# Hybrid attention and retention block: buffers for two tiles of x, an earlier second weight panel, the norm weights as a wide product

## The chip, the cores and the metric

The kernel runs on one core of a Trainium2 chip. The metric is the device time of one execution in microseconds (us), less is better. Before the change it takes 1588.69 us, the median of three runs (1588.14 to 1590.66).

## The reference

One residual layer over x of shape (1, 2048, 1024), float32. Cut to what matters:

```python
h = rms_norm(x, norm_gain)                       # x * rsqrt(mean(x*x) + eps) * norm_gain
aq, ak, av, ag, rq, rk, rv, rg = split(h @ w_in) # 1024 columns in, eight groups out
attn = window_attention(aq, ak, av, ...)         # 16 heads of 64, 4 kv heads, RMS norm on q and k,
                                                 # chunks of 64, window of 2 chunks, a sink per head
ret  = retention(rq, rk, rv, ...)                # 8 heads, chunks of 64, a state carried along the
                                                 # sequence, group norm per head
mixed = concat(attn * silu(ag), ret * silu(rg))  # 2048 wide
return x + mixed @ w_out                         # 2048 rows of 1024
```

Everything in it is computed in full; outputs are float32.

## The kernel before, in words

**Precision.** Each float32 operand of a projection is split into a high part H and a low part L (`fp32r`), and each product is three TensorE passes: H by H (L1441), L by H and H by L (L1442, L1443). Of a tile of x, ScalarE makes the high part (`xh`, L715) and VectorE the low part (`xl`, L1153); of a weight, ScalarE makes the high part (`wh1`, L531) and GpSimd the low part (`wl1`, L387). The norm weights (`ngain`) are applied in `xh` and `xl` as a scale per partition, so both work on one 128x128 piece at a time, 8 pieces a tile. The factor 1/rms of each row is applied later, at the eviction of a projection; `xsq` squares and sums the rows of x on ScalarE (L697), `xms_` and `xpow` make the power on VectorE and GpSimd, `XB` transposes it on TensorE.

**Tiling.** Four blocks of 512 rows (tiles t = 0 to 3 of 128 rows), and in each four head units, so units n = 0 to 15. A unit has 20 jobs of 24 matmuls each (`job(n, j)`): 0 to 3 make q, k and v for one tile each, with a tile of x as the moving or stationary side (384 wide, weight panel 0); 4 to 7 the gates and the retention's q and k (panel 1; they need all four tiles of x), 8 to 11 the retention's v and gate (panel 2), 12 to 19 the output projection (panel 3). Three PSUM banks go round among the jobs. Between the jobs stand the small pieces of the two mixers: `TQ` transposes q and k of a tile after their norm (L1460), `S_` makes scores (L1476), `PT` and `PV` the transposed probabilities and their product with v (L1500), `A` and `I` the retention inside a chunk with its state (L1538 to L1540), `MT` the transposed retention output.

**Weights.** In block 0 each panel comes from DRAM in four chunks through `stage` (three buffers, and `sx` for the fourth chunk of the first panel). A chunk is split by `wh1` and `wl1` (two steps each, numbered s = 0 to 7 in a panel), then `save` writes both parts to scratch in DRAM, and later blocks only `reload` them. `load(q)` waits on `s_wl`, the count of finished `wl1` steps, until its buffer is free.

**x.** The transposed tile lies in `xt[:, t % 2]`, two buffers, so tiles 2 and 3 wait for `xl` of tiles 0 and 1. `first_rows(t)` brings the untransposed rows of block 0 into `acc`. In block 0 all DMA starts are issued by SyncE's queue (SP) in a written order: norm weights, x and weight chunks in turn, tile 1, rows 0, identity; then tile 2 (waits), rows 1, tile 3 (waits), the gains of q and k, `attention_constants` (bias and the sinks), `load(4)`, rows 2, `load(5)`, rows 3, `load(6)`, `load(7)`, the saves.

**Order.** The order on every engine is written out by hand, unit by unit (GpSimd from L434, ScalarE from L718, VectorE from L1158, TensorE from L1564). An engine takes its instructions strictly in that order, so a wait of one holds all behind it. TensorE's order begins: job(0,0), job(0,1), job(0,2), TQ(0,0), job(0,3), S_(0,0), job(0,4), TQ(0,1), XB(0), job(0,5). ScalarE's: the first weight panel between the pieces of tile 0, tiles 1 and 2 with `xsq(0,0)` and `xsq(0,1)` between, the eviction `qkv(0,0)`, tile 3, and only then `wh1` of panel 1. VectorE's `carry_in(0)` stands ahead of `qk_norm(0,0)` and reads the sinks.

Of the kernel before, what the change touches and what calls it, by code (L numbers as in the profile page):

```python
# [94 lines left out]
def build(nc, x, norm_gain, q_gain, k_gain, sinks, ret_gain, xT, wp0, wp1, wp2, wp3, c_bias, c_ret, c_ident, out):  # L95
# [9 lines left out]
    with ExitStack() as ctx:  # L105
# [272 lines left out]
        def _(pool):  # L378
# [62 lines left out]
            ggm(0, 0); wl1(1, 0, 3); ggm(0, 1); wl1(1, 0, 4); mixl(0, 2); wl1(1, 0, 5); wl1(1, 0, 6)
            wl1(1, 0, 7); mixl(0, 3); gpow(0, 0); ggm(0, 2); wl1(0, 3, 0); wl1(0, 3, 1); wl1(0, 3, 2)
            wl1(0, 3, 3); gpow(0, 1); ggm(0, 3); wl1(0, 3, 4)

            rpow(1, 0); wl1(0, 3, 5); wl1(0, 3, 6); wl1(0, 3, 7); gpow(0, 2); rpow(1, 1); rpow(1, 2)
            wl1(1, 1, 0); gpow(0, 3); wl1(1, 1, 1); wl1(1, 1, 2); rpow(1, 3); wl1(1, 1, 3); wl1(1, 1, 4)
            wl1(1, 1, 5); wl1(1, 1, 6); wl1(1, 1, 7); wl1(1, 2, 0); wl1(1, 2, 1); wl1(1, 2, 2); wl1(1, 2, 3)
# [1283 lines left out]
```

## Time and profile before

| | before |
|---|---|
| median of three runs | 1588.69 us |
| profiled execution | 1589.65 us |
| its span | 1587.9 us |
| TensorE busy | 1560.4 us (98%) |
| VectorE busy | 1113.1 us (70%) |
| ScalarE busy | 853.2 us (54%) |
| GpSimd busy | 451.4 us (28%) |
| mean DMA rate | 204 GB/s |

The span is the stretch that the profile covers; the execution's own time is 1.75 us longer. A busy share is an average over all stages. In the views, PE is TensorE, DVE is VectorE, ACT is ScalarE, POOL is GpSimd, SPq is SyncE's queue of DMA starts; L and a number is the line of the kernel before. In a timeline row the columns are the start and the duration in us, the engine, line and operation, output and inputs with shapes, the count; in square brackets how long the engine stood idle before it and what ended that. Where an operation has a count above one, the duration is of the whole run of them.

### The profile page before, as it was taken

How to read it: one execution, taken by the hardware profiler on the slowest of the kernel's cores; microseconds unless marked ns; L12 is line 12 of the kernel's file. 1: busy time of each engine (PE TensorE's matmuls, PEld its weight loads, DVE VectorE, ACT ScalarE, POOL GpSimd, SP SyncE). 2: the span in 40 equal slices, each digit the busy share in tenths (PEclk: the TensorE clock that was granted, in tenths of full speed). 3: DMA queues.
4: the chain of work that ended last, by engine and by line, in shares of the span. 5: the costliest groups of instructions: out<-in, count | busy, mean ns of one | idle time of the engine just before them, and what ended most of it. 6: DMA issues, size and time to landing. Idle time of an engine off the chain costs nothing.

```text
span 1587.9 us, 24908 instructions
## 1 busy us (share of the span) xinstructions
PE 1560.4 (98%) x8120; PEld 1354.2 (85%) x8120; DVE 1113.1 (70%) x2934; ACT 853.2 (54%) x2421; POOL 451.4 (28%) x453
## 2 busy tenths in 40 slices
PE   6899999999999999999999999999999999999999
PEld 5798888978889888898888989889898888988887
DVE  6879587796946758576775766857587584775764
ACT  7766565655635355454754645546474454535641
POOL 5565566643312021120212212121120211202210
PEclk9999999999999999999999999999999999999999
DMA  7987495755874445553556635526447455444451
GB/s 260 330 315 280 175 345 186 285 208 178 323 256 166 188 146 188 186 209 145 186 215 225 247 128 195 205 99 247 168 159 282 148 197 189 149 179 156 154 207 54
DMA packets 123328, 323.66 MB, mean 204 GB/s; under 512 B 16832, under 2 KB 60224, under 8 KB 123200
## 3 DMA queue, kind: packets, MB, share of 16 engines
q1 hardware_dynamic: 123200, 322.07, 55.5%
q8 instruction: 66, 1.08, 0.3%
q14 instruction: 62, 0.51, 0.1%
HBM read 250.72 MB, written 71.30 MB: 203 GB/s over the span
## 4 chain that ended last, share of the span: by engine, by line
PE 84%; DVE 9%; issue 3%; ACT 2%; DMA 1%; POOL 1%; SPq 0%; DVEq 0%; POOLq 0%; ACTq 0%
PE jb L1441 24%; PE jb L1443 24%; PE jb L1442 24%; PE ob L1500 2%; PE s L1476 2%; PE ptb L1485 2%; PE ob L1460 1%; PE s L1539 1%; DMA stage<-wp_dram 1%; PE s L1538 1%; DVE hTL L1153 1%; PE ab L1550 1%; DVE acc L1139 1%; PE s L1377 1%; DVE qS L955 1%
## 5 line engine op out<-in xcount | busy, mean ns | idle before, releaser
L1441 PE MATMUL jb<-wH,hTH 128*128 128x512 f32 (+1 forms) x1024 | 376.6, 368 | 9.4 <-POOL wL L387 9.4
L1442 PE MATMUL jb<-wL,hTH 128*128 128x512 f32 (+1 forms) x1024 | 372.6, 364 | 0.0
L1443 PE MATMUL jb<-wH,hTL 128*128 128x512 f32 (+1 forms) x1024 | 372.3, 364 | 0.0
L1441 PEld LDWEIGHTS jb<-wH,hTH 128*128 128x128 f32 x1024 | 193.3, 189 | 30.0 <-POOL wL L387 11.9
L1443 PEld LDWEIGHTS jb<-wH,hTL 128*128 128x128 f32 x1024 | 193.3, 189 | 20.5
L1442 PEld LDWEIGHTS jb<-wL,hTH 128*128 128x128 f32 x1024 | 193.7, 189 | 17.6
L1441 PE MATMUL jb<-wH,mxH 128*128 128x512 f32 x512 | 207.6, 405 | 0.0
L1441 PE MATMUL jb<-hTH,wH 128*128 128x512 f32 x512 | 202.7, 396 | 2.8 <-POOL wL L387 2.8
L1443 PE MATMUL jb<-wH,mxL 128*128 128x512 f32 x512 | 200.6, 392 | 0.0
L1442 PE MATMUL jb<-wL,mxH 128*128 128x512 f32 x512 | 200.3, 391 | 0.0
L1442 PE MATMUL jb<-hTL,wH 128*128 128x512 f32 x512 | 199.7, 390 | 0.0
L1443 PE MATMUL jb<-hTH,wL 128*128 128x512 f32 x512 | 199.5, 390 | 0.0
L589 ACT ACTIVATE sx<-sx,nm 128x128 f32<-128x128 f32 x256 | 99.9, 391 | 160.9 <-DVE d L988 160.7
L412 POOL TENSOR_TENSOR mxL<-mixr,mxH 128x256 fp32r<-128x256 f32 x64 | 47.8, 747 | 465.4 <-ACT mxH L651 464.3
L387 POOL TENSOR_TENSOR wL<-stage,wH 128x512 fp32r<-128x512 f32 (+1 forms) x126 | 156.5, 1265 | 68.3 <-ACT wH L531 68.0
L1441 PEld LDWEIGHTS jb<-hTH,wH 128*128 128x128 f32 x512 | 96.2, 188 | 22.9 <-POOL wL L387 4.5
L1443 PEld LDWEIGHTS jb<-wH,mxL 128*128 128x128 f32 x512 | 96.1, 188 | 21.0
L1443 PEld LDWEIGHTS jb<-hTH,wL 128*128 128x128 f32 x512 | 96.1, 188 | 20.7
L1442 PEld LDWEIGHTS jb<-hTL,wH 128*128 128x128 f32 x512 | 96.3, 188 | 18.1
L1442 PEld LDWEIGHTS jb<-wL,mxH 128*128 128x128 f32 x512 | 96.6, 189 | 16.5
L1441 PEld LDWEIGHTS jb<-wH,mxH 128*128 128x128 f32 x512 | 96.3, 188 | 16.5
L394 POOL TENSOR_TENSOR rstd<-ms,mhalf 128x5 f32<-128x5 f32 x64 | 75.9, 1186 | 113.6 <-DVE ms L932 113.5
(142 smaller groups left out, 3016.6 us busy)
## 6 DMA issues: line engine op xcount, KB each, us to landing
wH<-scrH SPq DMA_DIRECT2D x144, 512.0 KB, 7.0
wL<-scrL SPq DMA_DIRECT2D x144, 512.0 KB, 7.9
stage<-wp_dram SPq DMA_DIRECT2D x48, 512.0 KB, 6.6
scrH<-wH SPq DMA_DIRECT2D x48, 512.0 KB, 6.5
scrL<-wL SPq DMA_DIRECT2D x48, 512.0 KB, 7.5
wH<-scrH SPq DMA_DIRECT2D x48, 384.0 KB, 5.5
wL<-scrL SPq DMA_DIRECT2D x48, 384.0 KB, 6.6
out_dram<-acc SPq DMA_DIRECT2D x16, 512.0 KB, 2.8
```

The lines of the kernel that those rows point to most:

```text
L387: pool.tensor_tensor(wL[b][:, s, 0:w], stage_of(at // 2, w)[:, s % 2], wH[b][:, s, 0:w].bitcast(F32), ALU.subtract).then_inc(S["s_wl"], 1)
L394: pool.tensor_tensor(rstd[:, t % 2], ms[:, t % 2], mhalf[:, 0:5], ALU.pow).then_inc(S["s_rstd"], 1)
L412: pool.tensor_tensor(mxL[:, 0:2, cols], mixr[:, :, :], mxH[:, 0:2, cols].bitcast(F32), ALU.subtract).then_inc(S["s_mixl"], 1)
L589: act.activation(v, v, ACT.Exp, bias=nm4[:, t % 2, i:i + 1], accum_out=den[:, t % 2, i:i + 1])
L955: v.scalar_tensor_tensor(out=qS[other, t % 2, :, a * 64:a * 64 + 64], in0=tr[rows, 0:256].rearrange("p (c q) -> p c q", q=64), scalar=qkg[ ...
L1139: v.tensor_tensor(a, a, bank_of(n, J_OUT + i)[:, :], ALU.add).then_inc(S["s_acc"], 1)
L1441: pe.matmul(o, lh, rh_, start=i == 0, stop=False)
L1442: pe.matmul(o, lh, rl_, start=False, stop=False)
L1443: m = pe.matmul(o, ll, rh_, start=False, stop=i == last)
L1476: m = pe.matmul(s_parts[:, par, hp], qS[:, t % 2, 2 * hp + par], kHL[:, :, win], start=True, stop=True)
L1485: m = pe.transpose(ptb[:, i * P:(i + 1) * P], sx[:, at:at + P], ident[:, :])
L1500: m = pe.matmul(o, v, pT[:, par * 256:(par + 1) * 256].rearrange("p (r q) -> p r q", q=64), start=i == 0, stop=i == 1)
```

## The change

- Tiles 2 and 3 of block 0 get own buffers (`xt23`, in the memory that `mxL` takes later), so their DMAs wait for nothing.
- For all tiles but the first, VectorE multiplies the tile by the norm weights in place (`xg`, two instructions of 128x512 a tile); `xh` is then a plain copy, and `xl` a plain subtraction, two of 128x512 each. Tile 0 keeps the old form.
- The four chunks of the first panel are started from ScalarE's queue, ahead of its first activation. SP's order is new: rows 0 to 3 and loads 4 to 6 come ahead of the gains and the attention constants; load 6 waits only for the first `wl1` pair.
- Panel 1 of unit 0 is split directly behind panel 0 on GpSimd (seven of its eight steps), on ScalarE between the pieces of x; TensorE runs job(0,0) to job(0,4) without anything between, then TQ(0,0), XB(0).
- The orders of all engines in all units are new. In TensorE's, units 6, 7, 9, 10, 11, 13, 14 and 15 have job(n,2) ahead of I(n-1,3); in unit 15, TQ(15,1) stands behind job(15,4) and I(15,2) behind job(14,13); unit 8 keeps its order there.

```diff
+        with nc.sbuf_tensor("xt23", [P, 2, KT, P], F32) as xt23:
+            pass
+        mxL, mxH = sb("mxL", [P, 4, BLK], F32R), sb("mxH", [P, 4, BLK], F32R)
+        def x_tile(b, t):
+            return xt23[:, t - 2] if b == 0 and t >= 2 else xt[:, t % 2]
...
             def load(q):
-                if q >= STAGES + 1:
-                    sp.wait_ge(S["s_wl"], 2 * (q - STAGES) + 2)
+                if q > STAGES:
+                    sp.wait_ge(S["s_wl"], 2 * (0 if q == 6 else q - STAGES) + 2)
...
             for c in range(4):
                 sp.dma_start(xt[:, 0, 2 * c:2 * c + 2], xT[0, 0, :, 2 * c:2 * c + 2]).then_inc(s_xp[c], 16)
-                load(c)
             x_turned(0, 1)
             first_rows(0)
+            x_turned(0, 2)
             sp.dma_start(ident[:, :], c_ident).then_inc(S["s_ident"], 16)
-            x_turned(0, 2)
+            load(6)
             first_rows(1)
+            load(4)
             x_turned(0, 3)
-            qk_gains()
+            load(5)
+            first_rows(2)
+            first_rows(3)
+            for half in range(2):
+                rows = slice(half * HD, half * HD + HD)
+                sp.dma_start(qkg[rows, 0:1], q_gain.rearrange("(d o) -> d o", o=1)).then_inc(S["s_qkg"], 16)
+                sp.dma_start(qkg[rows, 1:2], k_gain.rearrange("(d o) -> d o", o=1)).then_inc(S["s_qkg"], 16)
             attention_constants(0)
-            load(4)
-            first_rows(2)
-            load(5)
-            first_rows(3)
-            load(6)
             load(7)
...
# ScalarE
+                act.wait_ge(S["s_xg"], 8 * b + 2 * (t - 1) + c + 1)
+                ks = slice(4 * c, 4 * c + 4)
+                act.activation(hTH[:, ks, t * P:(t + 1) * P], x_tile(b, t)[:, ks], ACT.Copy).then_inc(S["s_xH"], 1)
+            for q in range(4):
+                act.dma_start(stage_of(q, W_WIDTH[0]), wp[0][0, :, 2 * q:2 * q + 2, :]).then_inc(s_stage(q), 16)
...
             xh(0, 0, 0); wh1(0, 0, 0); wh1(0, 0, 1); xh(0, 0, 1); wh1(0, 0, 2); wh1(0, 0, 3); xh(0, 0, 2)
+            wh1(0, 0, 4); wh1(0, 0, 5); xh(0, 0, 3); wh1(0, 0, 6); wh1(0, 0, 7); xsq(0, 0); xh(0, 1, 0)
+            xsq(0, 1); xh(0, 1, 1); wh1(0, 1, 0); wh1(0, 1, 1); xh(0, 2, 0); wh1(0, 1, 2); wh1(0, 1, 3)
+            wh1(0, 1, 4); xh(0, 2, 1)
+            qkv(0, 0); xsq(0, 2); wh1(0, 1, 5); xsq(0, 3); xh(0, 3, 0); wh1(0, 1, 6); xh(0, 3, 1); wh1(0, 1, 7)
...
# VectorE
+            def xg(b, t, c):
+                part = x_tile(b, t)[:, 4 * c:4 * c + 4]
+                v.tensor_tensor(part, part, ngain[:, 4 * c:4 * c + 4].unsqueeze(2).broadcast_to([P, 4, P]), ALU.mult
+                                ).then_inc(S["s_xg"], 1)
+            xl(0, 0, 0); xl(0, 0, 1); xl(0, 0, 2); xl(0, 0, 3); xg(0, 1, 0); xg(0, 1, 1); xl(0, 1, 0)
+            xg(0, 2, 0); xl(0, 1, 1); xms_(0, 0); xg(0, 2, 1); xl(0, 2, 0); xl(0, 2, 1); xg(0, 3, 0)
+            xg(0, 3, 1); xl(0, 3, 0); xl(0, 3, 1); xms_(0, 1); carry_in(0); v_parts(0, 0); xms_(0, 2)
...
# GpSimd
+            wl1(0, 0, 7); wl1(0, 1, 0); xpow(0, 0); wl1(0, 1, 1); wl1(0, 1, 2); wl1(0, 1, 3); wl1(0, 1, 4)
+            wl1(0, 1, 5); wl1(0, 1, 6); xpow(0, 1); xpow(0, 2)
+            rpow(0, 0); xpow(0, 3); rpow(0, 1); wl1(0, 1, 7); rpow(0, 2); rpow(0, 3); wl1(0, 2, 0); wl1(0, 2, 1)
...
# TensorE
-            job(0, 0); job(0, 1); job(0, 2); TQ(0, 0); job(0, 3); S_(0, 0); job(0, 4); TQ(0, 1); XB(0)
-            job(0, 5); S_(0, 1); TQ(0, 2); job(0, 6); S_(0, 2); TQ(0, 3); PT(0, 0); job(0, 7); S_(0, 3)
+            job(0, 0); job(0, 1); job(0, 2); job(0, 3); job(0, 4); TQ(0, 0); XB(0); job(0, 5); TQ(0, 1)
+            S_(0, 0); job(0, 6); TQ(0, 2); S_(0, 1); job(0, 7); TQ(0, 3); S_(0, 2); PT(0, 0); job(0, 8)
...
-            job(6, 0); I(5, 2); MT(5, 0); job(6, 1); I(5, 3); job(6, 2); TQ(6, 0); MT(5, 1); job(6, 3)
+            job(6, 0); I(5, 2); MT(5, 0); job(6, 1); job(6, 2); I(5, 3); TQ(6, 0); MT(5, 1); job(6, 3)
...
-            job(15, 0); I(14, 2); MT(14, 0); job(15, 1); I(14, 3); MT(14, 1); job(15, 2); TQ(15, 0); job(15, 3)
-            TQ(15, 1); MT(14, 2); job(15, 4); S_(15, 0); MT(14, 3); TQ(15, 2); job(15, 5); S_(15, 1); TQ(15, 3)
+            job(15, 0); I(14, 2); MT(14, 0); job(15, 1); job(15, 2); MT(14, 1); I(14, 3); TQ(15, 0); job(15, 3)
+            job(15, 4); TQ(15, 1); MT(14, 2); S_(15, 0); job(15, 5); TQ(15, 2); MT(14, 3); S_(15, 1); job(15, 6)
```

## Rows read from the trace of the kernel before

**Rows 1.** Windows by stage: length, busy us per engine, granted clock, DMA share, GB/s.
```profile
0.00:45.00 45.00, 31.36 (x141) 26.35 (x142) 31.90 (x82) 34.13 (x91) 26.71 (x29) 0.96 0.79 274
45.00:100.00 55.00, 51.82 (x271) 43.50 (x270) 45.96 (x91) 34.84 (x96) 32.79 (x32) 1.00 0.84 297
100.00:500.00 400.00, 397.39 (x2090) 345.73 (x2090) 303.12 (x749) 228.29 (x633) 194.04 (x176) 1.00 0.68 248
500.00:1460.00 960.00, 957.85 (x5000) 834.06 (x4999) 652.46 (x1799) 501.16 (x1445) 177.78 (x195) 1.00 0.50 184
1460.00:1588.00 128.00, 121.99 (x626) 104.61 (x624) 79.69 (x217) 54.81 (x158) 20.10 (x23) 0.99 0.40 151
```
**Rows 2.** Waits of TensorE, 0 to 45 us: total us, times, longest.
```profile
PE jb L1441 <- POOL wL L387: 11.4, 7, 8.1
```
**Rows 3.** Timeline of TensorE, 8 to 45 us.
```profile
15.84 0.33 PE L1441 MATMUL jb<-wH,hTH 128*128 128x384 f32 x1
...
23.99 0.34 PE L1443 MATMUL jb<-wH,hTL 128*128 128x384 f32 x1
26.60 0.90 PE L1460 MATMUL ob<-ident,rawqn 128*128 128x128 f32 x3 [2.28 <-DVE rawqn L946]
27.16 0.67 PE L1441 MATMUL jb<-wH,hTH 128*128 128x384 f32 x1
...
30.05 0.34 PE L1441 MATMUL jb<-wH,hTH 128*128 128x384 f32 x1
...
43.49 0.47 PE L1441 MATMUL jb<-hTH,wH 128*128 128x512 f32 x1
```
**Rows 4.** Timeline of GpSimd, first run of weight steps.
```profile
7.06 6.06 POOL L387 TENSOR_TENSOR wL<-stage,wH 128x384 fp32r<-128x384 f32 x6 [6.22 <-ACT wH L531]
```
**Rows 5.** Timeline of VectorE, 0 to 45 us.
```profile
7.65 8.71 DVE L1153 SCALAR_TENSOR_TENSOR hTL<-xt,ngain,hTH 128x128 fp32r<-128x128 f32 x12 [1.43 <-ACT hTH L715]
...
25.45 0.17 DVE L915 TENSOR_SCALAR nsink<-sink 128x2 f32<-128x2 f32 x1 [3.74 <-DMA sink<-sink_logits_dram]
```
**Rows 6.** Timeline of ScalarE, 16 to 32 us.
```profile
18.30 1.04 ACT L697 ACTIVATE gate<-acc 128x1024 f32<-128x1024 f32 x1
...
27.19 1.15 ACT L531 ACTIVATE wH<-stage 128x512 fp32r<-128x512 f32 x2 [3.71 <-DMA stage<-wp_dram]
```
**Rows 7.** Timeline of SyncE's queue, start of `load(4)`.
```profile
21.94 0.59 SPq L317 DMA_DIRECT2D stage<-wp_dram  x1
```
**Rows 8.** Window of 9 to 12 us, columns as in Rows 1.
```profile
9.00:12.00 3.00, 3.00 (x11) 2.46 (x9) 3.00 (x4) 2.72 (x8) 3.00 (x4) 1.00 1.03 417
```
**Rows 9.** Groups by line and form: count, duration ns min/median/max, start of first and last.
```profile
L715 ACT ACTIVATE hTH<-xt,ngain x128: 384/388/410, 5.1 to 1175.5; 128x128 fp32r<-128x128 f32 x128
...
L1153 DVE SCALAR_TENSOR_TENSOR hTL<-xt,ngain,hTH x128: 333/344/1449, 5.6 to 1177.4; 128x128 fp32r<-128x128 f32 x128
...
L899 DVE TENSOR_TENSOR pTL<-ptb,pTH x64: 675/684/693, 63.4 to 1554.9; 128x512 fp32r<-128x512 f32 x64
```
**Rows 10.** Timeline of TensorE, 45 to 75 us.
```profile
73.48 0.36 PE L1500 MATMUL ob<-pTH,veven 128*128 128x256 f32 x1 [1.22 <-DVE mixr L1028]
```
**Rows 11.** Timeline of VectorE, 45 to 60 us.
```profile
53.84 1.21 DVE L988 TENSOR_TENSOR d<-nm,sink 128x4 f32<-128x4 f32 x1
```
**Rows 12.** Timeline of TensorE, unit 6 and unit 8.
```profile
597.25 0.34 PE L1443 MATMUL jb<-wH,hTL 128*128 128x384 f32 x1
597.83 0.35 PE L1538 MATMUL s<-rst,zst 128*128 128x256 f32 x1 [0.24 <-issue]
...
795.71 0.36 PE L1538 MATMUL s<-rst,zst 128*128 128x256 f32 x1 [0.28 <-issue]
```
**Rows 13.** Timeline of VectorE around 597 us.
```profile
597.09 0.42 DVE L899 TENSOR_TENSOR aL<-amr,aH 128x256 fp32r<-128x256 f32 x1
```
**Rows 14.** Timeline of TensorE, unit 15.
```profile
1480.59 0.52 PE L1460 MATMUL ob<-ident,rawqn 128*128 128x128 f32 x3 [0.71 <-DVE kHL L960]
...
1537.16 0.36 PE L1538 MATMUL s<-rst,zst 128*128 128x256 f32 x1 [1.13 <-DVE kwL L899]
```

More of the change, by code:

```diff
@@ L441, in _ @@
[L441 to L447, printed above, removed]
@@ L789, in _ @@
-            gnx(5, 1); rvg(5, 3)
-            qkv(6, 0); kwh_ah(5, 3); ocopy(5, 2); v_shift(6, 0); rh(5, 3); mth(5, 0); qkv(6, 1); gnx(5, 2)
-            v_shift(6, 1); rh(6, 0); qkv(6, 2); ocopy(5, 3); tqh(6, 0); mth(5, 1); xsq(2, 2); v_shift(6, 2)
-            xsq(2, 3); qkv(6, 3); gnx(5, 3); tqh(6, 1); v_shift(6, 3); mth(5, 2); exps(6, 0); tqh(6, 2)
+                    for k in (2 * c, 2 * c + 1):
+                        i = act.activation(hTH[:, k, 0:P], x_tile(b, t)[:, k], ACT.Copy, scale=ngain[:, k:k + 1])
@@ new lines, in _ @@
+            pth(0, 3); gnx(0, 0); wh1(0, 3, 2); wh1(0, 3, 3); wh1(0, 3, 4); mixh(0, 2); kwh_ah(0, 2)
+            ocopy(0, 1); rh(0, 2); rvg(0, 3); wh1(0, 3, 5); obcopy(0, 3)
+            qkv(1, 0); mth(0, 0); gnx(0, 1); mixh(0, 3); v_shift(1, 0); rh(0, 3); ocopy(0, 2); kwh_ah(0, 3)
+            qkv(1, 1); wh1(0, 3, 6); mth(0, 1); wh1(0, 3, 7); v_shift(1, 1); gnx(0, 2); tqh(1, 0); ocopy(0, 3)
+            qkv(1, 2); wh1(1, 1, 0); wh1(1, 1, 1); wh1(1, 1, 2); wh1(1, 1, 3); v_shift(1, 2); xsq(1, 0)
@@ new lines, in _ @@
+            qkv(5, 0); mth(4, 0); ocopy(4, 2); v_shift(5, 0); qkv(5, 1); gnx(4, 2); v_shift(5, 1); xsq(2, 0)
+            qkv(5, 2); ocopy(4, 3); mth(4, 1); tqh(5, 0); xsq(2, 1); v_shift(5, 2); rh(5, 0); qkv(5, 3)
+            gnx(4, 3); v_shift(5, 3); tqh(5, 1); mth(4, 2); exps(5, 0); tqh(5, 2); mth(4, 3); exps(5, 1)
+            tqh(5, 3); pth(5, 0); exps(5, 2); obcopy(5, 0); pth(5, 1); ag(5, 0); exps(5, 3); ag(5, 1)
+            mixh(5, 0); obcopy(5, 1); rqh(5); pth(5, 2); mixh(5, 1); rqz(5); rk(5); obcopy(5, 2); mixh(5, 2)
@@ new lines, in _ @@
+            rvg(5, 0); pth(5, 3); kwh_ah(5, 0); rvg(5, 1); obcopy(5, 3); ocopy(5, 0); kwh_ah(5, 1); rh(5, 1)
+            mixh(5, 3); rvg(5, 2); gnx(5, 0); kwh_ah(5, 2); ocopy(5, 1); rh(5, 2); gnx(5, 1); rvg(5, 3)
+            qkv(6, 0); kwh_ah(5, 3); ocopy(5, 2); rh(5, 3); v_shift(6, 0); mth(5, 0); qkv(6, 1); gnx(5, 2)
+            v_shift(6, 1); qkv(6, 2); xsq(2, 2); ocopy(5, 3); v_shift(6, 2); tqh(6, 0); mth(5, 1); xsq(2, 3)
+            rh(6, 0); qkv(6, 3); gnx(5, 3); v_shift(6, 3); tqh(6, 1); mth(5, 2); exps(6, 0); tqh(6, 2)
@@ L830, in _ @@
[L830 to L831 removed]
+            qkv(10, 0); kwh_ah(9, 3); ocopy(9, 2); rh(9, 3); v_shift(10, 0); mth(9, 0); qkv(10, 1); gnx(9, 2)
+            v_shift(10, 1); qkv(10, 2); xsq(3, 2); ocopy(9, 3); v_shift(10, 2); tqh(10, 0); mth(9, 1); xsq(3, 3)
+            rh(10, 0); qkv(10, 3); gnx(9, 3); v_shift(10, 3); tqh(10, 1); mth(9, 2); exps(10, 0); tqh(10, 2)
@@ new lines, in xl @@
+            def xl(b, t, c):
+                v.wait_ge(S["s_xH"], x_done(b, t, c))
+                if b == t == 0:
+                    for k in (2 * c, 2 * c + 1):
+                        i = v.scalar_tensor_tensor(out=hTL[:, k, 0:P], in0=x_tile(b, t)[:, k], scalar=ngain[:, k:k + 1],
+                                                   in1=hTH[:, k, 0:P].bitcast(F32), op0=ALU.mult, op1=ALU.subtract)
+                    i.then_inc(S["s_xL"], 1)
+                    return
+                ks, cols = slice(4 * c, 4 * c + 4), slice(t * P, (t + 1) * P)
+                sub(hTL[:, ks, cols], x_tile(b, t)[:, ks], hTH[:, ks, cols]).then_inc(S["s_xL"], 1)
```

867 lines of the change are left out of this document (423 added, 444 removed).

## The prediction, made before the changed kernel ran

> **What bounds the kernel now.** I read the windows by stage first. TensorE is busy 957.85 of 960 us from 500 to 1460, and 397.39 of 400 before that [rows 1]. So work removed from other engines is worth nothing as such; only TensorE's idle time can be won: 13.64 us in the first 45 us, 3.18 from 45 to 100, 2.61 from 100 to 500, 2.15 from 500 to 1460, and 6.01 after 1460, part of it behind the last matmul. In the first 45 us the waits view gives 11.4 us to the weight low parts of GpSimd, 8.1 of them ahead of the first matmul and 3.3 in six later ones [rows 2]. The TensorE timeline has the other large wait, 2.28 us ahead of TQ(0,0), said to be for the normed q [rows 3]. VectorE's timeline says what it was: the instruction `nsink` stood 3.74 us for the sinks' DMA [rows 5], and all behind it on VectorE with it. After that wait TensorE was slow: from 27.16 to 30.05 nine matmuls of 384 columns take 0.32 us each, while from 15.84 to 23.99 forty-seven take 0.173 each [rows 3]. The granted clock, whose mean over the first stage is 0.96 [rows 1], stands at half of its 2.4 GHz there; nine times 0.148 is 1.3 us. The steady state loses a little in each unit at one place: I(n-1,3) starts 0.58 us after the matmul before it, where 0.17 is normal [rows 12], because `aL`, which it reads, ends at 597.51 [rows 13]. In unit 15 two waits of 0.71 and 1.13 idle us stand [rows 14].
>
> **Start, up to job(0,5): 3.2 us gained.** The first matmul depends on x chunk 0 and weight chunk 0. Both were issued by 2.3 us and the engines of the DMA moved what they could from 3 us on; I leave the start at 8.11. Eight steps of job(0,0) at GpSimd's pace of 1.01 us [rows 4] end at 15.84 as before. Then jobs 1 to 4 have nothing between, so what counts is when x and panel 1 are ready.
> The path: ScalarE has `xsq(0,1)` ahead of `xh(0,1,1)`, and it needs rows 1. Ahead of their last byte stand 4.8 MB (tile 0, four weight chunks of 0.39, tile 1, rows 0, tile 2, load 6, rows 1, 0.52 each). At 417 GB/s [rows 8] from 3 us they end at 14.5; at the stage's mean of 274 [rows 1] from 1 us at 18.4. I take the middle, 16.4. Then, with 1.1 us for a square [rows 6], 0.58 for a copy or weight split 512 wide (1.15 for two [rows 6]) and 0.69 for a 512 wide subtraction [rows 9]: xh(0,1,1) 18.1, xl(0,1,1) 18.8. The second half of job(0,1) is due at 17.9: 0.9 late. Load 4 lands 1.26 later than rows 1, tile 3 and load 5 behind it at 20.2; two splits, xh(0,2,0) 19.8, three splits from 20.2 to 21.9, xh(0,2,1) 22.5, its xl 23.2: job(0,2), from 20.9, has its half at 23.0, 0.2 late, and ends at 25.3. ScalarE goes on with qkv(0,0), 1.1 us by width, two squares and one split between: xh(0,3,0) 27.0, xl(0,3,0) 27.7. So job(0,3) waits 2.4 us, a new wait of about the old one's length, and I charge it the old one's slow clock, 1.3. It ends at 27.7 + 24 x 0.173 + 1.3 = 33.2; job(0,4) (24 of 0.173 x 512/384) at 38.7. The steps of GpSimd for panel 1, seven of 1.35 from 15.7, are done by 26: the 3.3 us of late low parts in job(0,4) go, and so does the wait for load 4, that was issued at 21.94 [rows 7] and left ScalarE idle 3.71 us [rows 6]. With TQ(0,0) and XB job(0,5) starts at 39.3 against 43.49 [rows 3]; 1.0 us of small TensorE work (S_(0,0), TQ(0,1)) has moved behind it: 3.2 gained. Bounds: with no wait but GpSimd's, job(0,4) ends at 33.9, gain 8; with rows 1 at 18.4 and xl(0,3,0) at 30, and VectorE and GpSimd holding each other up by 1.5 more, a gain of 0, and below it -1 for a second drop of the clock.
> The x work itself: ScalarE's 128 pieces of 388 ns become 8 and 30 wide ones of 0.58, 49.7 us against 20.5; VectorE's 128 of 344 (44) become 8, 30 products and 30 subtractions of 0.69 (44) [rows 9]. Both engines are idle enough after 100 us, so it is nothing there; the price in the first 30 us is in the path above. Twelve pieces took 8.71 us beside GpSimd's weight steps, 0.73 each against 0.344 alone [rows 5, 9]; a wide one takes that wait once rather than four times. By the Trainium skill, SBUF — State Buffer, section "SBUF: two separate sides", a VectorE instruction with two SBUF inputs and a GpSimd instruction that reads SBUF hold a shared port in turn, each for its whole length. The trace agrees: such pieces go at GpSimd's pace. Taken strictly, a wide instruction in that stretch waits for the rest of the GpSimd step that is under way.
>
> **ScalarE's queue.** It saves SyncE four starts of 0.4 to 0.6 us, so tile 1 is asked for some 2 us earlier, and they cost ScalarE as many, before its first input is there (idle until then): nothing, unless the chunks now compete with more of x. Bounds: 0.5 gained, 1 lost; I take 0. By the Trainium skill, DMA: Bandwidth & Descriptors, section "Issuing engines are not separate DMA queues", another issuing engine saves no more than the issue time. No run here shows a second issuer.
>
> **45 to 100 us: 1.2 gained of 3.18.** The wait at 73.48, 1.22 for `mixr` [rows 10], is VectorE's: it is busy 45.96 of 55 us [rows 1] and some tiny instructions take 1.21 us there beside GpSimd [rows 11]. Panel 1 has gone from GpSimd by then, so these get shorter, but tile 0's softmax, once in the first 45 us, now falls in. Bounds: -5 and +3.
>
> **100 to 500: 1.3 of 2.61.** Waits of TQ and PV for VectorE, in units whose TQ is now later by a job or so. Bounds -1.5 and +2.5.
>
> **500 to 1460 and after: 2.9.** I counted seven units (6, 7, 9, 10, 11, 13, 14) with I(n-1,3) behind job(n,1), each with a gap of 0.41. A job of 4.16 us now stands between, against which `aL` at 597.51 has ended long before; 7 x 0.41 = 2.9. Against it stands unit 8: it had the new order already and still has an idle 0.28 at 795.71 [rows 12], since VectorE had x pieces and the state update ahead of `aL`. If VectorE's new orders do the same the term is 0. They put fewer instructions ahead, so I take it whole.
>
> **After 1460: 1.8 of 2.3.** The same gap in unit 15, 0.4; TQ(15,1) gets a job before it (0.71), I(15,2) another (1.13) [rows 14]. I leave 0.4 to a new wait. Bounds 0 and 2.5.
>
> **Sum.** 3.2 + 1.2 + 1.3 + 2.9 + 1.8 = 10.4 off the profiled execution's 1589.65: 1579.3. That execution lies 0.96 above the median of the runs, so by the median it is 1578.3. I forecast 1579.
>
> **Rivals.**
> (a) Only the order of TensorE's late pieces pays. Evidence: the first 45 us are bound by the DMA (0.79 share, 417 GB/s where it peaks [rows 1, 8]), and moving rows ahead moves x back. The start gives 0, 45 to 500 gives 0.5, the rest 4.7: -5.2, 1584. Against it: the waits at 21.94 to 27 are SyncE's order, not the rate.
> (b) All early waits go: 8 + 2.5 + 2 + 2.9 + 2.2 = 17.6, 1572. For it: the bytes suffice if rows 1 land at 14.5 and ScalarE's squares fit. Against it: five ScalarE instructions stand between qkv(0,0) and tile 3.
> (c) Slower: VectorE becomes the bound from job(0,5) to 100 us. TQ(0,0) comes 12 us later than at 26.60, so the softmax of tile 0 (four wide ones of 0.68 and five small ones, up to 1.21 each beside GpSimd, 5.8 in all) and 1.3 of q and k fall behind 45 us, where VectorE has 9.0 idle, and that in pieces between TensorE's results. If none is usable TensorE is 7.1 later, with two slow stretches of 1.3: 9.7; the 1.2 and 1.3 of the next terms are lost. 3.2 + 2.9 + 1.8 - 9.7 = -1.8, and with the start at 0 it is -5: 1591 to 1594, say 1592. It decides once VectorE's waits in that stretch exceed the present ones by 8. Against it: the softmax of before didn't stand on TensorE's path there.
> (d) No change: the start gives 0 and VectorE's order brings unit 8's wait to every unit; what is left is the 1.8 at the end, less something: 1587.5.
>
> **How the numbers follow.** Forecast 0.46, (a) 0.19, (b) 0.11, (c) 0.12, (d) 0.12. The band of 0.2% (about what a measurement of this kernel can tell from no change) is 3.2 us, 1585.5 to 1591.9. The forecast, (b) and most of (a) are below it: 0.74. (d) and a part of (a) and (c) are in it: 0.17. The rest of (c) is slower: 0.09. The range, 1573.5 to 1588, takes in the forecast's bounds, (a) and half of (d), and leaves out (c) and the far end of (b).
>
> **What would show it.** Right: in the new trace job(0,5) starts near 39.3; a wait of about 2.4 ahead of job(0,3) ended by VectorE's or ScalarE's tile 3, and matmuls of 0.52 after it; none for the low parts in job(0,4); I(n-1,3) of units 6 to 14 without idle time. Wrong: rows 1 landing after 19 us, waits of TensorE for VectorE over 5 us between 45 and 100, or idle time unchanged at I(n-1,3).

## The result and the profile after

The changed kernel takes 1573.5 us (median of four executions, 1573.34 to 1574.11) against 1589.6 for the kernel before beside it (1588.14 to 1590.66): ratio 0.9898, 95% interval 0.9882 to 0.9914. It is 16.1 us faster, where the forecast's sum was 10.4, and 1573.5 lies on the lower edge of the range. The sign was right and the term for the start was near; the other four terms were each too small by 1.4 us or more.

The windows of the changed kernel by stage (columns as in [rows 1]):

```profile
0.00:45.00 45.00, 32.02 (x150) 27.50 (x151) 33.35 (x62) 28.81 (x65) 30.92 (x31) 1.00 0.90 324
45.00:100.00 55.00, 54.14 (x299) 47.34 (x298) 48.40 (x105) 37.11 (x104) 35.35 (x32) 1.00 0.83 299
100.00:500.00 400.00, 398.08 (x2109) 348.97 (x2108) 308.60 (x744) 231.22 (x623) 192.22 (x176) 1.00 0.67 247
500.00:1460.00 960.00, 960.00 (x5024) 839.67 (x5024) 663.84 (x1783) 490.23 (x1407) 183.25 (x198) 1.00 0.51 186
1460.00:1572.00 112.00, 107.79 (x546) 91.59 (x545) 70.40 (x182) 45.91 (x134) 16.11 (x18) 1.00 0.36 135
```

From 500 to 1460 us TensorE is now busy all 960 us, where 2.15 were idle, and yet more than 2.15 us were gained there. That is the first thing to see. TensorE's records overlap: a matmul of 0.33 us is followed by the next after 0.17. So the idle time before a late one is about 0.16 us less than what it loses. The starts are the better measure. In both kernels the jobs stand in the same order; this table has the start of the first matmul of some jobs, read from both timelines:

| job | before | after | difference |
|---|---|---|---|
| (0,0) | 8.11 | 9.89 | +1.78 |
| (0,3) | 27.16 | 29.09 | +1.94 |
| (0,4) | 33.40 | 33.52 | +0.12 |
| (0,5) | 43.49 | 39.78 | -3.71 |
| (0,9) | 74.93 | 67.47 | -7.47 |
| (1,2) | 106.42 | 100.39 | -6.03 |
| (2,0) | 194.73 | 190.44 | -4.28 |
| (5,1) | 496.69 | 487.95 | -8.73 |
| (6,0) | 587.80 | 579.11 | -8.69 |
| (15,0) | 1459.67 | 1446.56 | -13.11 |
| last job's end | 1584.11 | 1567.79 | -16.31 |

At the marks from (0,3) to (0,9) less small work has been done in the changed kernel than before; at the others both have done the same. The gain falls between (1,2) and (2,0): the changed kernel has three new waits there.

TensorE's timeline of the changed kernel, the places that answer to [rows 3] (L1469 to L1471 are now the three passes):

```profile
9.89 0.69 PE L1469 MATMUL jb<-wH,hTH 128*128 128x384 f32 x1 [9.89 <-POOL wL L396]
...
18.62 0.44 PE L1469 MATMUL jb<-wH,hTH 128*128 128x384 f32 x1 [0.36 <-DVE hTL L910]
...
29.09 0.41 PE L1469 MATMUL jb<-wH,hTH 128*128 128x384 f32 x1 [1.88 <-DVE hTL L910]
...
39.78 0.48 PE L1469 MATMUL jb<-hTH,wH 128*128 128x512 f32 x1
...
117.50 0.52 PE L1488 MATMUL ob<-ident,rawqn 128*128 128x128 f32 x3 [1.01 <-DVE kHL L973]
119.05 0.50 PE L1469 MATMUL jb<-wH,mxH 128*128 128x512 f32 x1 [0.56 <-ACT rawqn L550]
...
128.09 0.50 PE L1469 MATMUL jb<-wH,mxH 128*128 128x512 f32 x1 [0.35 <-DVE acc L1152]
```

The start is 1.8 us late, job(0,3) waits 1.88 us for tile 3, and none of job(0,4)'s four waits for GpSimd is left. The last three rows are the new waits. The rows of ScalarE and VectorE say why the start and job(0,3) are late:

```profile
6.27 1.28 ACT L723 ACT_TABLE_LOAD   x1 [6.27 <-DMA xt<-xT_dram]
...
16.59 0.63 ACT L728 ACTIVATE hTH<-xt 128x512 fp32r<-128x512 f32 x1 [2.23 <-DVE xt L1170]
...
18.17 0.61 ACT L728 ACTIVATE hTH<-xt 128x512 fp32r<-128x512 f32 x1
...
26.62 0.61 ACT L728 ACTIVATE hTH<-xt 128x512 fp32r<-128x512 f32 x1
```

```profile
23.78 3.49 DVE L1170 TENSOR_TENSOR xt<-xt,ngain 128x512 f32<-128x512 f32 x2
27.27 3.37 DVE L910 TENSOR_TENSOR hTL<-xt,hTH 128x512 fp32r<-128x512 f32 x2
...
770.65 1.29 DVE L1170 TENSOR_TENSOR xt<-xt,ngain 128x512 f32<-128x512 f32 x2
```

The first part of x, which landed at 3.80 us before, is there at 6.27. The four chunks of weights are now started from 0.73 us on from another queue, beside and partly ahead of it; the first experiment shows that this is the reason. A wide product takes 0.65 us at 770, where GpSimd has no weight step, and 1.74 at 23.78 beside its weight steps.

I(5,3) starts 0.17 us behind the last matmul of job(6,2), where it started 0.58 behind that of job(6,1) [rows 12]:

```profile
592.72 0.33 PE L1471 MATMUL jb<-wH,hTL 128*128 128x384 f32 x1
592.89 0.28 PE L1566 MATMUL s<-rst,zst 128*128 128x256 f32 x1
593.01 0.28 PE L1567 MATMUL s<-rv,aH 128*128 128x256 f32 x1
```

### The profile page after: what moved, and what is told of

Same layout as the page of the kernel before. It is cut to its first block, busy times and chain, and to the rows that moved or that the text cites. A ratio compares the mean times of both kernels' runs of the same rounds, so it can differ in the third digit from the quotient of the medians.

```text
span 1571.6 us, 24771 instructions
## 1 busy us (share of the span) xinstructions
PE 1552.0 (99%) x8120; PEld 1355.1 (86%) x8120; DVE 1124.6 (72%) x2874; ACT 833.3 (53%) x2331; POOL 457.9 (29%) x453
## 4 chain that ended last, share of the span: by engine, by line
PE 92%; DVE 4%; POOL 1%; DMA 1%; issue 1%; ACT 1%; SPq 0%; DVEq 0%; ACTq 0%; POOLq 0%
PE jb L1469 26%; PE jb L1470 26%; PE jb L1471 26%; PE ob L1528 2%; PE s L1504 2%; PE ptb L1513 2%; PE ob L1488 1%; PE s L1567 1%; PE ab L1578 1%; PE s L1566 1%; POOL wL L396 1%; PE s L1405 1%; DMA stage<-wp_dram 1%; PE ab L1405 0%; PE ab L1407 0%
## 5 line engine op out<-in xcount | busy, mean ns | idle before, releaser
L1469 PE MATMUL jb<-wH,hTH 128*128 128x512 f32 (+1 forms) x1024 | 376.3, 367 | 13.0 <-POOL wL L396 10.7
L1471 PE MATMUL jb<-wH,hTL 128*128 128x512 f32 (+1 forms) x1024 | 372.3, 364 | 0.0
L1469 PEld LDWEIGHTS jb<-wH,hTH 128*128 128x128 f32 x1024 | 193.0, 188 | 33.6 <-POOL wL L396 12.4
L1471 PEld LDWEIGHTS jb<-wH,hTL 128*128 128x128 f32 x1024 | 193.1, 189 | 20.4
L1469 PE MATMUL jb<-wH,mxH 128*128 128x512 f32 x512 | 207.1, 405 | 0.9 <-ACT rawqn L550 0.6
L1469 PE MATMUL jb<-hTH,wH 128*128 128x512 f32 x512 | 201.4, 393 | 0.0
L1471 PE MATMUL jb<-wH,mxL 128*128 128x512 f32 x512 | 200.6, 392 | 0.0
L1471 PE MATMUL jb<-hTH,wL 128*128 128x512 f32 x512 | 199.7, 390 | 0.0
L1471 PEld LDWEIGHTS jb<-wH,mxL 128*128 128x128 f32 x512 | 96.2, 188 | 21.1
L1471 PEld LDWEIGHTS jb<-hTH,wL 128*128 128x128 f32 x512 | 96.2, 188 | 20.5
L1469 PEld LDWEIGHTS jb<-hTH,wH 128*128 128x128 f32 x512 | 96.3, 188 | 18.9 <-ACT rawqn L550 0.3
L1469 PEld LDWEIGHTS jb<-wH,mxH 128*128 128x128 f32 x512 | 96.4, 188 | 18.2 <-ACT rawqn L550 0.8
```

The lines of the kernel that those rows point to most:

```text
L1469: pe.matmul(o, lh, rh_, start=i == 0, stop=False)
L1471: m = pe.matmul(o, ll, rh_, start=False, stop=i == last)
```

## The experiments

**The chunks back on SyncE's queue.**

```diff
             for c in range(4):
                 sp.dma_start(xt[:, 0, 2 * c:2 * c + 2], ...)
+                load(c)
-            for q in range(4):
-                act.dma_start(stage_of(q, W_WIDTH[0]), ...)
```

> The changed kernel, with the first four weight chunks started again by SyncE's queue, in turn with the four parts of tile 0, and none by ScalarE's. Theory (the chunks on ScalarE's queue are ahead of x part 0, whose landing went from 3.80 to 6.27 us, and that is what moved the first matmul from 8.11 to 9.89): the first matmul is at 8.1 again; but the path of tile 3 is set by ScalarE and by VectorE beside GpSimd, which all start 1.8 us earlier too, so the execution is 1.0 to 1.8 us shorter than the changed kernel, 1572. Rival (the chunks' place pays for itself, since the start then runs against the landing of rows 1 and tile 3): first matmul at 8.1, but the wait ahead of job(0,3) grows from 1.88 by as much, TensorE's clock falls again, and the time is 1573.5 or up to 1575.

Measured: 1574.32 us (1573.16 to 1574.85), not to be told from the changed kernel's. The first matmul is at 7.45 again, sooner even than the 8.1 of theory and rival; the time is the rival's. The first row of ScalarE, then rows of TensorE:

```profile
3.80 1.28 ACT L724 ACT_TABLE_LOAD   x1 [3.80 <-DMA xt<-xT_dram]
```

```profile
7.45 0.69 PE L1467 MATMUL jb<-wH,hTH 128*128 128x384 f32 x1 [7.45 <-POOL wL L397]
...
19.80 0.45 PE L1467 MATMUL jb<-wH,hTH 128*128 128x384 f32 x1 [1.26 <-DVE hTL L908]
...
25.14 0.44 PE L1467 MATMUL jb<-wH,hTH 128*128 128x384 f32 x1 [0.67 <-DVE hTL L908]
30.30 0.49 PE L1467 MATMUL jb<-wH,hTH 128*128 128x384 f32 x1 [2.80 <-DVE hTL L908]
```

The first matmul is 2.4 us sooner, and all of it is lost again in the middle of job(0,1) and of job(0,2) and ahead of job(0,3), which starts 1.2 us later than in the changed kernel, and with the clock at its lower level for part of it (granted clock 0.58 from 30 to 33 us). ScalarE's queue costs the first matmul 2.4 us and costs the kernel nothing that can be measured.

**I(n-1,3) back in its old place**, eight units.

```diff
-            job(6, 0); I(5, 2); MT(5, 0); job(6, 1); job(6, 2); I(5, 3); TQ(6, 0); ...
+            job(6, 0); I(5, 2); MT(5, 0); job(6, 1); I(5, 3); job(6, 2); TQ(6, 0); ...
```

> The changed kernel, with I(n-1,3) of units 6, 7, 9, 10, 11, 13, 14 and 15 put back between job(n,1) and job(n,2); nothing else. Theory (the place of I(n-1,3) is the whole of what the steady state gained): each of the eight units has its wait of 0.4 us again, the time is 8 x 0.40 = 3.2 us longer, 1576.7. Rival (the new orders of VectorE and ScalarE made aL come earlier): under 1 us longer, 1573.5 to 1574.5. Second rival (more than the wait hangs on it, since the switch between a job and a small piece costs TensorE something each time): 8 x 0.5 = 4 us or more.

Measured: 1578.07, 4.6 us longer, as much as the second rival says. From the start of job(6,0) to the end 4.7 come back: eight times about 0.53, and one new wait at 906 that loses 0.47. In unit 6:

```profile
588.89 0.34 PE L1471 MATMUL jb<-wH,hTL 128*128 128x384 f32 x1
589.52 0.36 PE L1566 MATMUL s<-rst,zst 128*128 128x256 f32 x1 [0.29 <-issue]
589.72 0.28 PE L1567 MATMUL s<-rv,aH 128*128 128x256 f32 x1
```

From start to start it is 0.63 us, 0.46 more than normal. The other 0.07 or so is inside I(5,3): behind the wait its second matmul starts 0.20 after the first, where it is 0.12 in the changed kernel. The second rival's reason, a price of each switch between a job and a small piece, isn't seen: the step from I(5,3) to job(6,2) takes no longer than the one from I(5,3) to TQ(6,0) in the changed kernel (0.12 both).

**The same move in the kernel before.**

```diff
-            job(6, 0); I(5, 2); MT(5, 0); job(6, 1); I(5, 3); job(6, 2); TQ(6, 0); ...
+            job(6, 0); I(5, 2); MT(5, 0); job(6, 1); job(6, 2); I(5, 3); TQ(6, 0); ...
```

> The kernel before, with only this changed in TensorE's order: in the same eight units I(n-1,3) (in unit 15 with MT(14,1)) stands behind job(n,2) instead of ahead of it. Theory: 8 x 0.40 = 3.2 us shorter than before, 1586.4, with no idle time at these places. Rival (the wait follows, as in unit 8 of the kernel before, which has this order and waited 0.28 idle us nevertheless): within 1 us of before, 1589. Against more than 3.2: the other units' orders are those of before.

Measured: 1594.69, slower: ratio 1.0028 (1.0018 to 1.0038). Neither theory nor rival. In most of the middle units the 0.4 goes and a wait ahead of TQ(n,1) comes that loses 0.24, so about 0.2 is gained. In unit 15 this comes:

```profile
1482.59 0.87 PE L1460 MATMUL ob<-ident,rawqn 128*128 128x128 f32 x3 [4.62 <-DVE kHL L960]
...
1484.97 0.63 PE L1441 MATMUL jb<-hTH,wH 128*128 128x512 f32 x1
```

VectorE's old order has the state and norm of I(14,3) ahead of the q and k statistics. I(14,3) came a job later, so these did too, and TQ(15,1) waited 4.62 us. The matmuls after it ran 0.43 apart instead of 0.23, the clock at its lower level (granted clock 0.50 from 1482 to 1488 us). So the move pays 0.5 a unit with the changed kernel's orders of the other engines, and less than nothing with the old ones.

This run shows one thing more. Up to unit 6 its code is that of the kernel before, and yet it takes 1.1 us less from job(2,0) to job(6,0) in its profile (391.9 for 393.1): the losses of the kernel before at 260 us (0.66) and at 407 us (0.30) aren't there. So differences of about 1 us in this stretch come from one execution to the next.

**x in narrow pieces again**, the norm weights as a scale.

```diff
-                act.activation(hTH[:, ks, ...], x_tile(b, t)[:, ks], ACT.Copy)
+                for k in range(4 * c, 4 * c + 4):
+                    i = act.activation(hTH[:, k, ...], x_tile(b, t)[:, k], ACT.Copy, scale=ngain[:, k:k + 1])
```

VectorE's product is left out, and its subtraction works on pieces again.

> The changed kernel, with the norm weights applied again inside the high and low parts of x, eight 128x128 pieces a tile on ScalarE and eight on VectorE, and no product of its own on VectorE; the orders stay. Theory (the wide form is bought for the blocks after the first and the start: ScalarE 1.6 us a tile instead of 1.2, VectorE pieces that each wait for a GpSimd step): in the first 30 us TensorE waits 2 us more ahead of jobs 1 to 3, elsewhere nothing: 1575.5. Rival (VectorE gains from the missing product, twelve wide instructions beside GpSimd in the start, each up to 1.7 us): the wait ahead of job(0,3) is gone, and the time is 1571.5. Third: the units before blocks 1 to 3 (3, 7, 11), where the kernel before had waits at 804 and 1191 us, get them back: another 0.5 to 1 us.

Measured: 1579.56 (1576.35 to 1581.77), 6 us longer, with executions 5.4 us apart. The profiled execution is the longest of them, 8.4 above the changed kernel's. By its starts 2.9 is there at job(0,9), near what the theory has, 0.1 in units 8 and 12 each, and 5.3 in unit 4, at one place that none of the three named. TensorE's row, then one of ScalarE's from before it:

```profile
405.24 0.35 PE L1563 MATMUL s<-rHL,rqH 128*128 128x256 f32 x1 [3.44 <-DVE aL L915]
```

```profile
390.54 1.15 ACT L541 ACTIVATE wH<-stage 128x512 fp32r<-128x512 f32 x2 [3.63 <-DMA stage<-wp_dram]
```

The weight chunk for which ScalarE stands here is issued at 384.44, in SyncE's order behind a tile of x that waits for the low parts; that is 2.1 us later than in the changed kernel, the shift of 2.9 taken off. VectorE then stands 4.83 us for ScalarE. It is not in every execution: the shortest, 1576.35, is 2.9 us above the changed kernel, which the start alone gives. That the narrow pieces start this chain is read from one trace, and not shown.

**Two buffers for x.**

```diff
         def x_tile(b, t):
-            return xt23[:, t - 2] if b == 0 and t >= 2 else xt[:, t % 2]
+            return xt[:, t % 2]
```

SyncE's order: tile 2 behind load 4, tile 3 behind rows 2.

> The changed kernel, with tiles 2 and 3 of block 0 in the two old buffers: their DMAs wait for the low parts of tiles 0 and 1, and stand in SyncE's order where that wait is short (tile 2 behind load 4, tile 3 behind rows 2). Theory (the own buffers are not what gains): in the changed kernel VectorE takes tile 2 at 18.49 us and tile 3 at 23.78, and the last low part of tile 0 is done at 15.1, of tile 1 at 19.8, so both tiles land in time or up to 1 us late; the first job behind them shifts by at most 1, and VectorE's pace behind job(0,5) takes that up: 1573.5 to 1574.5. Rival (the buffers matter): tile 2 lands at 18.5 or later, VectorE stands with xl(0,1,1) behind it, each of jobs 1 to 3 waits, two slow stretches of the clock: 1576 or more.

Measured: 1579.16, 5.7 longer, which is the rival's number. TensorE's rows, then ScalarE's:

```profile
22.27 0.45 PE L1466 MATMUL jb<-wH,hTH 128*128 128x384 f32 x1 [1.17 <-DVE hTL L910]
...
30.62 0.41 PE L1466 MATMUL jb<-wH,hTH 128*128 128x384 f32 x1 [1.81 <-DVE hTL L910]
...
35.44 0.69 PE L1466 MATMUL jb<-wH,hTH 128*128 128x384 f32 x1 [1.84 <-DVE hTL L910]
```

```profile
32.86 0.63 ACT L541 ACTIVATE wH<-stage 128x512 fp32r<-128x512 f32 x1 [3.70 <-DMA stage<-wp_dram]
```

VectorE gets the tiles at 20.9 and 26 us, some 2 later than in the changed kernel; job(0,3) starts 1.5 later for it. The larger part comes inside job(0,3), 4.1 us, and is made by what stands behind the waiting SyncE: load 7, issued at 27.56 instead of 23.33. ScalarE stands 3.70 us for it, with tile 3's second half behind, and TensorE's clock is at its lower level meanwhile (granted clock 0.50 from 33 to 37 us).

**The whole DMA side as before**, orders as changed.

```diff
             sp.dma_start(ident[:, :], c_ident).then_inc(S["s_ident"], 16)
-            load(6)
+            x_turned(0, 2)
             first_rows(1)
-            load(4)
             x_turned(0, 3)
...
             attention_constants(0)
+            load(4)
+            first_rows(2)
+            load(5)
+            first_rows(3)
+            load(6)
             load(7)
```

> The changed kernel with the whole DMA side of the start as before: two buffers for x, chunks on SyncE's queue in turn with x, tile 2 and 3 waiting, gains and constants ahead of loads 4 to 6. The orders of the engines and the wide product stay. Theory (what the early second panel is bought with is SyncE's order): load 4 is issued at about 22 us again and lands at 27, so ScalarE, which now has the splits of panel 1 ahead of tile 3, makes tile 3 only at 30 to 33, job(0,3) waits 6 to 8 us, and of this 3 to 6 us stay at the end: 1577 to 1580. Rival (VectorE's pace from job(0,5) to 70 us takes up even that): 1575 or less.

Measured: 1584.7, 11.2 longer, more than the theory had. Load 4 is issued at 25.25. The wait stands ahead of job(0,2) and not of job(0,3), since two splits of panel 1 are ahead of tile 2 in ScalarE's order. ScalarE's row, then TensorE's:

```profile
30.46 1.15 ACT L542 ACTIVATE wH<-stage 128x512 fp32r<-128x512 f32 x2 [10.80 <-DMA stage<-wp_dram]
```

```profile
33.04 0.69 PE L1464 MATMUL jb<-wH,hTH 128*128 128x384 f32 x1 [10.23 <-DVE hTL L908]
```

**The new DMA side in the kernel before.** The same edit the other way round, with the own buffers; the first chunks stay on SyncE's queue.

> The kernel before with the DMA side of the change alone: own buffers for tiles 2 and 3, SyncE's order with loads 4 to 6 and all rows ahead of the gains and constants; the first chunks stay on SyncE's queue, the orders of all engines and the narrow x pieces stay. The reverse of the run with the old DMA side. Theory (the DMA side removes the wait of ScalarE for load 4, 3.71 us, but TQ(0,0) stands ahead of job(0,3) and waits for the sinks, which are issued at about 20 us in either): the wait of 2.3 stays within 1 us, the 3.3 us of late low parts in job(0,4) shrink to under 1, total 2 to 4 us shorter than before, 1586. Rival (the DMA side is worth its 11.6 us here too, since it is what the start waits for): 1578. Second rival (VectorE's pace behind job(0,5) takes up the gain): 1588 to 1589.

Measured: 1587.14 against 1589.59 (ratio 0.9991, 0.9982 to 1.0000; executions 1585.49 to 1591.44): the theory's lower end at best. In its profile, that of the longest execution, 2.06 us are won at job(0,5) and kept, and 3.7 are lost in unit 8, where VectorE waits for the sinks' DMA and TensorE for VectorE:

```profile
787.19 0.17 DVE L924 TENSOR_SCALAR nsink<-sink 128x2 f32<-128x2 f32 x1 [4.43 <-DMA sink<-sink_logits_dram]
```

So the DMA side is worth 0 to 3 us with the old orders and 11 with the new; the parts of this change don't add.

**VectorE's carry_in later, in the kernel before.**

```diff
-            ... gnm(7, 1); carry_in(8); xl(2, 3, 0); ...
-            mtl(7, 0); qk_stats(8, 1); ...
+            ... gnm(7, 1); xl(2, 3, 0); ...
+            mtl(7, 0); carry_in(8); qk_stats(8, 1); ...
```

> The kernel before, with VectorE's carry_in(8) and carry_in(12), which read the sinks, behind mtl(7,0) and mtl(11,0), where the changed kernel has them (with the wait of qk_norm on s_mixr that the changed kernel has in its place); nothing else. In the kernel before, VectorE stands 1.97 us for the sinks' DMA at 787, and in the profile with the new DMA side 4.43, behind which TensorE waited 2.9 at 793 with a slow stretch: 3.7 us in one place. Theory (this wait, of a length that changes from one execution to the next, is a part of what the changed kernel gained in units 8 and 12, and why executions of the kernel before lie 5 us apart and those of the changed one 0.8): 0.5 to 1.5 us below before, 1588.5, with executions within 1.5 us of each other and less idle time at I(7,3) and I(11,3). Rival (the scatter comes from the start, where the clock falls or does not after the wait of 2.3): median and spread as before.

Measured: 1587.26 against 1589.78 (ratio 0.9984, 0.9975 to 0.9993), more than the theory had. By the starts 0.8 us are won in unit 8 and 0.2 in unit 12, where the waits of the kernel before are gone. Another 1.4 differ ahead of unit 5, where the same losses are missing as in the run with I(n-1,3) moved in the kernel before, whose code is unchanged there; so these need not be this edit's. Eight of eleven executions lie within 1.2 us, the others up to 2.5 above: the sinks are at most a part of the scatter.

**TQ(15,1) and I(15,2) back in their old places.**

```diff
-            job(15, 4); TQ(15, 1); MT(14, 2); S_(15, 0); job(15, 5); ...
+            TQ(15, 1); MT(14, 2); job(15, 4); S_(15, 0); job(15, 5); ...
-            job(14, 12); A(15, 3); PV(15, 1); job(14, 13); MT(15, 0); I(15, 2); ...
+            job(14, 12); A(15, 3); I(15, 2); PV(15, 1); job(14, 13); MT(15, 0); ...
```

> The changed kernel, with TQ(15,1) again right behind job(15,3) and I(15,2) right behind job(14,12). Theory: the two waits of before return, 0.87 and 1.29 us: 2.0 us longer, 1575.5. Rival (VectorE's new order of unit 15 has taken the waits away too): under 0.7 longer. Second rival (as in the kernel before with one piece moved, VectorE's order now does not match, and the wait of TQ(15,1) is 3 us or more with a slow stretch behind it): 1578 or more.

Measured: 1574.51, 1.0 longer, between theory and first rival. TQ(15,1) loses 0.53 again (0.87 before), PV(15,3) 0.35, and I(15,2) nothing where it had lost 1.29: the new orders of the other engines had taken that wait away already.

**TensorE's old order in units 2 and 3 alone.**

```diff
-            job(2, 0); I(1, 2); MT(1, 0); job(2, 1); job(2, 2); I(1, 3); MT(1, 1); job(2, 3); TQ(2, 0)
+            job(2, 0); job(2, 1); I(1, 2); MT(1, 0); job(2, 2); TQ(2, 0); MT(1, 1); job(2, 3); I(1, 3)
```

> The changed kernel with TensorE's order in units 2 and 3 as before (the other engines' orders as changed). From job(2,0) to job(4,0) the changed kernel takes 194.3 us and the kernel before 197.9. Theory (the gain of 100 to 500 us lies in TensorE's order, two small pieces side by side instead of each between two jobs, and later TQ): 2 to 3.6 us come back, 1576. Rival (as at unit 15: orders that don't match cost more than either): over 4 us, 1578 or more, with a wait of over 2 us somewhere. Second rival (the new order of VectorE makes it): under 1 us.

Measured: 1631.33, 58 us longer. TensorE's waits from 190 to 440 us (total, times, longest), the first four:

```profile
PE ob L1528 <- DVE pTL L910: 9.8, 2, 5.7
PE s L1504 <- DVE kHL L973: 8.7, 2, 4.5
PE ob L1488 <- DVE rawqn L959: 7.3, 2, 4.2
PE ob L1528 <- DVE mixr L1041: 4.8, 3, 3.2
```

Six of the seven waits above 3 us are followed by a stretch at the lower clock. This is the first rival, far beyond its number. Which engine's order makes the gain of these units can't be read from it.

**ScalarE's squares of unit 1 behind the eviction.**

```diff
-            ... v_shift(1, 2); xsq(1, 0); xsq(1, 1); mth(0, 2); qkv(1, 3); tqh(1, 1); ...
+            ... v_shift(1, 2); mth(0, 2); qkv(1, 3); xsq(1, 0); xsq(1, 1); tqh(1, 1); ...
```

> The changed kernel, with ScalarE's two squares xsq(1,0), xsq(1,1) of unit 1 behind qkv(1,3) instead of ahead of it. Theory (TensorE's 0.71 us ahead of job(0,14) at 118 us is ScalarE's eviction of job(1,3), 2.2 us late for the two squares): the wait is gone, and with it part of the next (0.59): 0.7 to 1.3 us shorter, 1572.5. Rival (the softmax of unit 1 on VectorE is next and as late): no change beyond 0.3.

Measured: 1572.17 (1572.06 to 1572.31), 1.3 less than the changed kernel, as the theory had it at its upper end, and faster than both kernels. The changed kernel has a wait of 0.56 us for ScalarE ahead of job(0,14) (the row at 119.05 above), and with the squares later the job starts at 118.31 without a wait; the wait at 128 is gone too.

**Tile 3 sooner**, on top of it.

```diff
-            qkv(0, 0); xsq(0, 2); wh1(0, 1, 5); xsq(0, 3); xh(0, 3, 0); ...
+            qkv(0, 0); xsq(0, 2); wh1(0, 1, 5); xh(0, 3, 0); xsq(0, 3); ...
-            xl(0, 2, 0); xl(0, 2, 1); xg(0, 3, 0); xg(0, 3, 1); ...
+            xl(0, 2, 0); xg(0, 3, 0); xl(0, 2, 1); xg(0, 3, 1); ...
```

> The run with the squares later, 1572.17, and with tile 3 sooner: ScalarE takes xh(0,3,0) ahead of xsq(0,3), VectorE takes xg(0,3,0) ahead of xl(0,2,1). Theory (what is left of the start is taken up by VectorE's pace between job(0,5) and job(0,9); a start later by 1.4 us at job(0,5) had come back to 0 at job(0,9)): the wait ahead of job(0,3), 2.0, falls by 0.5 to 1.3, and the time by 0 to 0.3: 1572. Rival (the start still counts): 1571 or less. Third (the swap makes job(0,2) wait for xl(0,2,1) and a second wait comes): 1572.5 or more.

Measured: 1572.16, no change. Job(0,3) starts 1.2 sooner (27.88). Job(0,4) starts at 33.56, where the changed kernel has it (33.52): a wait for the second half of tile 3 and one for the eviction of job(0,1) have taken the gain. In the run with the squares later the same job started at 34.97, at the lower clock, and those 1.4 us are gone by job(0,9) (67.40 there, 67.58 here).

## Why the prediction came out as it did

The terms are compared at marks where both kernels have done the same work: job(1,2) at about 100 us, job(5,1) at about 490, job(15,0), the end.

| term | forecast | measured |
|---|---|---|
| start, up to job(0,5) | 3.2 | 2.7 |
| 45 to 100 us | 1.2 | 3.3 |
| 100 to 500 us | 1.3 | 2.7 |
| 500 to 1460 us | 2.9 | 4.4 |
| after 1460 us | 1.8 | 3.2 |
| sum | 10.4 | 16.3 |

The first two are parted by the forecast's estimate of 1.0 us for the small work that moved behind job(0,5).

- **What bounds the kernel**: right. VectorE's work grew by 11 us (1124.6 against 1113.1) while the kernel became 16 us faster. But TensorE's idle time in the windows fell by 7.6 us only, from 27.6 to 20.0. The step that failed first is here: "only TensorE's idle time can be won". It took the idle time of the view as the pool of each term. A late matmul loses 0.16 us more than its idle time, and slow matmuls count as busy.
- **The start**: near, and by luck. The first matmul was left at 8.11, with 1 us as the most that ScalarE's queue could lose; it came at 9.89. Job(0,0) took 8.7 us instead of 7.7. Against this, the late halves of tiles 1 and 2 (0.9 and 0.2) didn't come, nor in this execution the slow clock after the wait, 1.3. Job(0,5) started at 39.78 for 39.3, and xh(0,1,1) ended at 18.8 for 18.1, but not by rows 1: ScalarE stood for VectorE's product of tile 1, which started only at 15.06, behind the low parts of tile 0 beside GpSimd. The path of the prediction had no time for the products at all. Ahead of job(0,3), xh(0,3,0) ended at 27.2 for 27.0, and its subtraction took 1.7 us beside GpSimd where 0.69 had been put in; the wait was 1.88 for 2.4.
- **ScalarE's queue**: "I take 0" holds for the whole kernel, not for its reason. The Trainium skill, DMA: Bandwidth & Descriptors, "Issuing engines are not separate DMA queues", has all transfers interleave on the same DMA engines. The trace agrees, and shows the other side of it: chunks issued sooner delay what is needed first, by 2.5 us.
- **45 to 100 us**: the term that was off most, 1.2 for 3.3. The kernel before loses 4.0 us there by the starts, not the 3.18 of idle time. The prediction let VectorE take 2.0 back; the two waits for the softmax that came, at 52 and 66 us, lose 1.35. What is beyond the difference of these is not taken apart by any run.
- **100 to 500 us**: 1.3 for 2.7. The pool was mis-sized: the kernel before loses 4.2 us in waits there, not 2.61, and 1.0 of them isn't in another execution of the same code. That a good half would come back as new waits was right in kind: three new ones, at 117, 119 and 128 us, lose 2.5. They all stand ahead of job(2,0); from there to job(6,0) none came. The rest of the gain is spread, with 128 switches between jobs and small pieces instead of 144, and no run takes it apart.
- **500 to 1460 us**: 2.9 for 4.4. The mechanism was right. The seven units gave 3.5 together: 0.42 to 0.45 in five of them, 0.69 and 0.63 in units 7 and 11. Missed was unit 8, whose wait had been left in place: 0.8, all of which `carry_in` behind the sinks' DMA can give by the experiment with it.
- **After 1460**: 1.8 for 3.2. The 0.4 held back for a new wait was not needed, 0.71 idle was 0.87 lost and 1.13 idle was 1.29, and the other engines' orders did the part of I(15,2).
- **The wide product**: "nothing" after the start isn't safe. Narrow pieces with the new orders cost 5.3 us in unit 4 in one execution, and nothing there in another.
- **The rivals**: the time is nearest to (b), 1572, but not by its mechanism; the wait for tile 3 and the late start stayed. (c) didn't come: TensorE's waits for VectorE from 45 to 100 us were 0.9 us in all, where (c) wanted 8 more than before. (d) didn't come either: I(n-1,3) has no idle time in any of its units.

What stays open: how the gain of units 2 to 5 divides between TensorE's and VectorE's orders, and what part of it is the one profiled execution's.

## What to carry to other kernels

Measure a wait of an engine whose records overlap from start to start, not by its idle time, and compare two kernels only at marks where both have done the same work. Before a difference of 1 us in one trace is given to an edit, look whether another execution of the same code has it too. An order of one engine has its worth only with those of the others: the same move gained 0.5 us a unit with matching orders and made the kernel slower without them. When a queue waits, count what is issued behind it, and put what is needed first ahead of what is merely early, on whichever queue.
